# Forgetting keys, forgetting queries and memory queries by seven half-size products, zero rows in the score operands, and moved edges

## The reference, cut to what matters

```python
q_lat, c_kv, k_r, f_q, f_k, f_v, f_logit, m_q, g = jnp.split(h @ w_in, split_points, axis=-1)
...
s = jnp.einsum('bqhd,bkhd->bhqk', f_q, f_k).astype(jnp.float32) * FOX_SCALE      # forgetting branch
s = s + (jnp.swapaxes(c_q, 1, 2)[..., :, None] - jnp.swapaxes(c_k, 1, 2)[..., None, :])
...
s = jnp.einsum('bqhd,bmhd->bhqm', m_q, m_k).astype(jnp.float32) * MEM_SCALE      # memory branch
...
gates = jax.nn.sigmoid(g.astype(jnp.float32)).astype(h.dtype).reshape(b, s, N_BRANCH, D_MODEL)
...
x1 = layer_norm(ALPHA * h + mixer_out, ln1_g, ln1_b)
return layer_norm(ALPHA * x1 + moe_ffn(x1, *moe_w), ln2_g, ln2_b)
```

## Time and profile before

| what | us |
|---|---|
| median of three runs | 1115.58 |
| range of the runs | 1115.3 to 1116.18 |
| the profiled execution | 1115.3 |
| its span, first to last instruction | 1113.5 |
| PE busy in the span | 1085.7 |
| DVE busy | 494.0 |
| ACT busy | 180.4 |
| POOL busy | 87.5 |

### The profile page before, as it was taken

How to read it: one execution, slowest core, us unless ns; L and a number is a source line. 1 busy time by engine, 2 the same in 40 slices (tenths; PEclk the granted TensorE clock), 3 DMA queues, 4 the chain that set the end, 5 groups by cost and what they waited for, 6 DMA issues and landing times.

```text
span 1113.5 us, 16884 instructions
## 1 busy us (share of the span) xinstructions
PE 1085.7 (98%) x6302; PEld 655.1 (59%) x6302; DVE 494.0 (44%) x1285; ACT 180.4 (16%) x364; POOL 87.5 (8%) x103
## 2 busy tenths in 40 slices
PE   8999999999999999999999999999999999999994
PEld 4455569998777755476555545555555455555551
DVE  1130147777656333375564353343342442433435
ACT  1222124442222100010010100101101101101012
POOL 2112000000000000001034300000000000000000
PEclk9999999999999999999999999999999999999997
DMA  9632353523856578461899999999999999999971
GB/s 337 201 119 90 133 189 107 196 105 107 280 190 234 212 285 330 167 216 35 326 358 371 395 400 401 389 397 384 394 397 390 394 407 389 396 398 389 394 303 59
DMA packets 82330, 313.52 MB, mean 282 GB/s; under 512 B 13208, under 2 KB 24016, under 8 KB 56024
## 3 DMA queue, kind: packets, MB, share of 16 engines
q1 hardware_dynamic: 64864, 276.90, 63.6%
q0 software_dynamic: 7280, 16.44, 4.9%
q10 hardware_dynamic: 10128, 19.40, 4.9%
HBM read 306.24 MB, written 11.34 MB: 285 GB/s over the span
## 4 chain that ended last, share of the span: by engine, by line
PE 94%; DVE 3%; another core or an unknown queue 1%; issue 1%; ACT 0%; DMA 0%; ACTq 0%; DVEq 0%
PE ps_P L1346 20%; PE ps_V L1371 10%; PE ps_V L1360 10%; PE ps_P L1102 10%; PE ps_P L975 6%; PE ps_V L1282 6%; PE ps_S L1360 5%; PE ps_P L994 4%; PE ps_V L1291 4%; PE ps_T L1335 3%; PE ps_T L968 2%; PE ps_P L984 1%; PE ps_V L1323 1%; PE ps_P L1144 1%; PE ps_S L1353 1%
## 5 line engine op out<-in xcount | busy, mean ns | idle before, releaser
L1346 PE MATMUL ps_P<-arena,branch_out 128*64 128x256 f32 (+1 forms) x2176 | 233.6, 379 | 0.7 <-DVE branch_out L2047 0.7
L1346 PEld LDWEIGHTS ps_P<-arena,branch_out 128*64 128x64 f32 (+1 forms) x2176 | 152.0, 135 | 90.3 <-issue 19.3
L2068 DVE TENSOR_TENSOR branch_out<-branch_out,ps_P 128x256 f32<-128x256 f32 x33 | 13.9, 421 | 287.3 <-PE ps_P L1346 269.2
L1360 PE MATMUL ps_V<-weight_ring,branch_out 128*128 128x512 f32 x264 | 124.1, 592 | 0.0
L1371 PE MATMUL ps_V<-arena,branch_out 128*64 128x512 f32 (+1 forms) x544 | 120.6, 598 | 0.0
L1554 ACT ACTIVATE weight_ring<-ps_V,merge 128x512 f32<-128x512 f32 x66 | 45.3, 687 | 414.5 <-PE ps_V L1371 402.6
L2091 DVE TENSOR_TENSOR x_sb<-x_sb,ps_V 128x512 f32<-128x512 f32 x132 | 90.7, 687 | 17.4 <-PE ps_V L1360 17.2
L1371 PEld LDWEIGHTS ps_V<-arena,branch_out 128*64 128x64 f32 (+1 forms) x544 | 34.8, 135 | 77.2 <-issue 60.4
L1360 PEld LDWEIGHTS ps_V<-weight_ring,branch_out 128*128 128x128 f32 x264 | 47.9, 191 | 47.3 <-issue 47.3
L1360 PE MATMUL ps_S<-weight_ring,branch_out 128*128 128x512 f32 x132 | 67.4, 592 | 0.0
L1282 PE MATMUL ps_V<-branch_out,weight_ring 128*128 128x384 f32 x192 | 62.2, 487 | 0.5 <-DVE branch_out L1802 0.5
(11 more groups left out here) (354 smaller groups left out, 1233.4 us busy)
## 6 DMA issues: line engine op xcount, KB each, us to landing
arena<-w_e_gate SPq DMA_DIRECT2D x68, 1024.0 KB
arena<-w_e_up SPq DMA_DIRECT2D x68, 1024.0 KB
arena<-w_e_down SPq DMA_DIRECT2D x68, 1024.0 KB
weight_ring<-w_in SPq DMA_DIRECT2D x12, 1024.0 KB, 9.4
weight_ring<-w_in ACTq DMA_DIRECT2D x8, 1024.0 KB, 7.7
gates<-arena ACTq DMA_DIRECT2D x12, 384.0 KB, 3.2
arena<-fox_k_t SPq DMA_DIRECT2D x8, 512.0 KB, 3.8
arena<-cache_fox_v SPq DMA_DIRECT2D x8, 512.0 KB, 4.3
```

The lines of the kernel that those rows point to most:

```text
L1346: last = mm(bank[r:r + wide, 0:256], xgT[q][:, k, r:r + wide], w[h][:, k, :], start=(k == 0), stop=(k == KD - 1))
L1360: mm(tiles[k % 3][:, :], back[1 - q][:, (k // 2) * P:(k // 2 + 1) * P], yo[1 - q][:, (k % 2) * 512:(k % 2 + 1) * 512], start=True, stop=Tr ...
```

## The change

1. `fk`, `fq` and `mq` are computed by the same seven products as the gates: six more blocks (`HEADS_TWO`, `NH` = 6) at the front of the `W` numbering, back to back, with no attention steps between them. ACT moves each block's result to its place (`make_heads`). `fv` goes first, `fk` is feature-major at once, so `("T","fk",j)` and the DVE copies are gone; the output `fox_k` is stored feature-major from `fkA` and `fkS`, and the host turns it.
2. `inputs` runs right after the latents. The mixed inputs live in `x_sb`, so x is loaded only after the last gate product.
3. `("V","c","p")` moves from behind the `mk` transposes to between the six blocks and `qn`.
4. The rows of `krT`, `qrS`, `krTc` and of `fqA`, `fkA` that were not used are set once (zeros, and ones against zeros), and the score matmuls contract over all 128 rows. POOL does nine more clears at the start, and SP's wait `rows_set` goes from 4 to 11.
5. Half of `V out` 2 1 moves between the transposes of x1 block 0 and block 1 (`outpiece`); three eighths of `shpiece` 1 move ahead of `V rt` 1; `shact` is split in two.
6. At the end the three engines load the chunk count before their last pair, the two cases stand as `If` and `Else`, `pairs_over` is gone, the sums go in the order 0, 2, 4, 1, 3, 5 through three banks, and the first three wait for the first half of `yo` alone.

```diff
+HEADS_TWO = [(name, m) for name in ("fk", "fq", "mq") for m in range(2)]
+NH = len(HEADS_TWO)
...
-    s.append(("rms",))
-    s += [("P", "fk", j) for j in range(TT)]
+    s += [("inputs",), ("rms",)]
     s += [("P", "fv", j) for j in range(TT)]
+    s += [("weights", 0, m) for m in range(3)]
     s += [("T", "lat", j) for j in range(TT)]
-    s += [("P", "kn", 0), ("P", "kn", 1), ("P", "qr", 0), ("T", "fk", 0), ("P", "qr", 1), ("T", "fk", 1)]
-    s += [("P", "kn", 2), ("P", "kn", 3), ("T", "fk", 2), ("kcat",), ("qrope",)]
+    s += [("P", "kn", 0), ("P", "kn", 1), ("P", "qr", 0), ("P", "qr", 1), ("P", "kn", 2), ("P", "kn", 3), ("kcat",), ("qrope",)]
     s += [("P", "vm", j) for j in range(2)]
-    s += [("P", "fq", m) for m in range(4)]
+    for i in range(NH):
+        for r in range(7):
+            s.append(("W", i, r))
+            if r == 3:
+                s.append(("weights", i, 3))
+            elif r >= 4 and i + 1 < NH:
+                s.append(("weights", i + 1, r - 4))
+    s += [("V", "c", "p"), ("heads", NH - 1)]
...
-        mm(out[:, 0:keys], fqA[0:66, i, qs], fkA[0:66, i, 0:keys], start=True, stop=False)
+        mm(out[:, 0:keys], fqA[:, i, qs], fkA[:, i, 0:keys], start=True, stop=False)
...
-        mm(out[:, 0:PAST], qrS[0:RD, i, :], krTc[0:RD, :], start=False, stop=True)
+        mm(out[:, 0:PAST], qrS[:, i, :], krTc, start=False, stop=True)
...
-        last = mm(out[:, PAST:keys], qrS[0:MR, i, :], krT[0:MR, 256:T], start=False, stop=True)
+        last = mm(out[:, PAST:keys], qrS[:, i, :], krT[:, 256:T], start=False, stop=True)
...
+                if r == 0:
+                    if i == 0:
+                        pe.wait_ge(free["P"], done_at("P", "vm", 1))
...
+            def make_heads(i):
+                name, two = HEADS_TWO[i]
+                cells, ms = gate_two[i % 2], slice(2 * two, 2 * two + 2)
+                act.wait_ge(w_read, 7 * i + 7)
+                if name == "mq":
+                    last = fn(mqT[:, ms, :], cells, ACT.Copy, scale=MEM_SCALE)
+                else:
+                    heads, sample, scale = (fqA, fqS, FOX_SCALE) if name == "fq" else (fkA, fkS, 1.0)
+                    for r in range(2):
+                        fn(heads.rearrange("p (m r) c -> p m r c", r=2)[0:64, ms, r, :], cells[r * 64:(r + 1) * 64, :, 0:256], ACT.Copy, scale=scale)
+                    last = fn(sample[:, ms, :], cells[:, :, 256:T], ACT.Copy, scale=scale)
+                last.then_inc(heads_made, 1)
...
+            chunks_n = chunk_count(pe)
             step(PAIRS, 0, [(0, 32 * (PAIRS // 2 + 1)), (1, 32 * (PAIRS // 2 + 1))], quad=True)
-            with if_more(pe):
+            def last_sums(n):
+                pe.wait_ge(back_ready, n + 1)
+                pe.wait_ge(added, 6 * n + 6)
+                for m, k in enumerate(LAST_SUMS):
+                    pe.wait_ge(yo_ready, 2 * n + 1 + m // 3)
+                    if m >= 3:
+                        pe.wait_ge(last_added, m - 2)
...
+            with pe.If(chunks_n <= 4):
+                last_sums(FIXED)
+            with pe.Else():
```

More of the change, by code:

```diff
@@ L819, in _ @@
                 if n == 29:
+                    sp.wait_ge(done["W"], done_at("W", NH + TWO - 1, 6))
+                    for j in range(TT):
+                        sp.dma_start(x_sb[:, j, :], xs[j]).then_inc(x_loaded[j], 16)
                     sp.wait_ge(done["V"], done_at("V", "b", 0, 0, 0))
@@ L987, in latents @@
                             last.then_inc(done["P"], 1)
-            def feat_major(st, first, m):
-                out = bank(st)
-                for k in range(KD):
-                    if k % 4 == 0:
-                        slot = w_wait(first + k // 4)
-                    last = mm(out[:, 0:T], slot[:, k % 4, m * P:(m + 1) * P], xT[:, k, :], start=(k == 0), stop=(k == KD - 1))
-                last.then_inc(done["P"], 1)
             def scores(n):
@@ L1159, in _ @@
                         last = tr(out[0:RD, 3 * P:4 * P], kr_rot[:, j, :], P)
-                    elif key[0] == "fk":
-                        j = key[1]
-                        pe.wait_ge(free["P"], done_at("P", "fk", j))
-                        out = bank(st)
-                        for m in range(4):
-                            last = tr(out[:, m * P:(m + 1) * P], fk_tok[:, j, m * P:(m + 1) * P], P)
                     elif key[0] == "mk":
@@ L1284, in _ @@
                     elif key[0] == "out":
-                        _, j, half = key
-                        out = bank(st)
-                        for k in range(KD):
-                            pe.wait_ge(free["V"], done_at("V", "b", k // 4, 2, k % 4))
-                            if k % 4 == 0:
-                                slot = w_wait(first_of["out"] + half * 2 + k // 4)
-                            last = mm(out[:, :], yT[:, k, j * P:(j + 1) * P], slot[:, k % 4, :], start=(k == 0), stop=(k == KD - 1))
-                        last.then_inc(done["V"], 1)
+                        out_products(st, 4 if key[1:] == (TT - 1, 1) else 0, KD)
                     elif key[0] == "rt":
@@ L1566, in _ @@
                         pair(i * 2 + p + FIXED, 1 - p)
[L1567 to L1573 removed]
+                last_squares()
         @block.vector
@@ L1862, in _ @@
                 elif ring == "inputs":
[L1863 to L1865 removed]
+                    for loaded in lat_loaded:
+                        dve.wait_ge(loaded, 32)
                     x_dif, x_all, x_end, x_low = x_mix
```

272 lines of the change are left out of this document (143 added, 129 removed).

## The result

The changed kernel took 1097.21 us (median of four runs, 1096.8 to 1097.55) beside 1115.44 for the one before (four runs, 1112.93 to 1116.18); the ratio is 0.984, 95% interval 0.9823 to 0.9857. The forecast was 1097.9 with a range of 1094.5 to 1103. The profiled execution took 1096.8, its span is 1095.0 (1113.5 before): -18.5, where the steps of the prediction gave -17.65.

A forecast was written before the change was run, and what follows sets the result against it. PE was taken to bound the kernel nearly everywhere. Terms -6.4 (projections with edges), -6.3, -1.85, -3.5 and +0.4 sum to -17.65 from the profiled 1115.3 us: 1097.7, forecast 1097.9 for the runs' median, range 1094.5 to 1103.

The forecast's parts named there:

- rival E: More gain than forecast: key transposes save 1.3 us, `shd` and router waits all go, register load free; 1095.2 us, chance 0.12.
- Projections, -7.4: Key, forgetting-query and memory-query projections: 62.0 us of matmuls removed, 42 products of 1.30 us (54.6) added, without waits; -7.4 us.
- edges +1.0: Around the projections: key transposes 0, moved decay sums +0.7 at the first score, larger copies ahead of later `qn` +0.3 us.
- The +0.3 for the later `qn`: In the pattern `qn`, `mk`, `qa`: ACT's copy ahead has 512 columns instead of 384, +0.1 us three times.
- rival B: Dense projection products wait in each block for DVE or weights, 0.15 us a product, +6.3; 1104.2 us, chance 0.09.
- rival C: Projection products starve outright at 2.0 us each, making the kernel slower than before; 1127 us, chance 0.03.
- Zero rows, -6.3: First-branch scores of eight streams: full 128 rows avoid about 0.1 us on each side of every height change; 8 x -0.79.
- Rival A: Zero rows in the scores give nothing, as a switch costs on the columns' side alone; 1104.2 us, chance 0.10.
- Router, -1.85: Norm and router: second router piece 0.93 us earlier, wait at `shd` shrinks by 0.9; range -2.9 to 0.
- End, -3.5 + 0.4: Last sums start without PE's 2.09 us idle, at full clock, LN2 3.5 us earlier; PE's earlier register load costs 0.4.
- rival D: The change at the end does not pay, PE's branch stalling as long as the removed wait; 1101.4 us, chance 0.10.
- Experts, 0: Expert stage, about half the time: untouched, its loads started by PE's own progress; no change.

## Why the prediction was right, step by step

The total was 0.9 us off in the span, and the terms were right nearly one by one, with errors that cancel in part: the router gave 0.36 less, the end 0.76 more, and the first stretch 0.44 that no term had. Of rival E the free register load came true, but the key transposes saved nothing and the router less than forecast.

- **Projections, -7.4 and edges +1.0.** Measured: 62.0 removed, 54.84 added, -7.2. From the first block to the first product, keys left out, nothing changed by the chain of waits (31.27 against 51.88 - 20.60 = 31.28): the key transposes had stood where PE would have waited for ACT. The edge behind the products cost +0.77 (39.25 us from the last of them to the first score, against 38.48 without the memory queries), as much as the wait for the first score grew. The +0.3 for the later `qn` is there too (brackets of 0.26 us, and 0.11 more than before from the start of a `qa` to the next `qn`, three times), but behind the last `qa` 0.36 us went, which I had not counted. No product behind the first ever waited, so rival B and rival C are out; the added DVE work shows how far off C was. The first stretch was 0.44 shorter: 0.05 because PE's first product started at 4.24 instead of 4.29, the rest in the next few. In every profile the first four recorded instructions take about 0.75 us each and later ones of the same shape 0.36; when the faster pace sets in differs from run to run, and with it the first of the 42 products (54.42 to 55.51 in the nine profiles that share this code). What sets it off is not known, and the change need not have a part in it, since two profiles of the kernel before differ by 0.83 us there.
- **Zero rows, -6.3.** -6.24, shown alone in the old kernel. Rival A is out. My price of 0.1 us on each side of a change was right, as 0.19 a change. The 66-row products gave nothing that shows, as counted: 8 x 0.78 (1.99 - 1.31, and 0.10 at the gate product) is already the whole 6.24. The later load of x cost nothing either, since this stage, which holds the gates, takes 213.05 us with it and without.
- **Router, -1.85.** -1.49 (1.46 up to `shd` and 0.03 behind it). The step that was mis-sized is the second router piece, forecast at -0.93: it came 0.58 earlier (51.05 us behind the first output product instead of 51.63). The three shared products before it take 1.30 us, more than the wait of 0.94 that they cover, so they delay it by the difference; I had followed the transposes and not PE. The mask followed by -0.64, with a wait of 1.08 where I expected 1.3. `shd` gave -0.82 for the -0.9 expected.
- **End, -3.5 + 0.4.** -3.86, so rival D is out. PE's register load costs nothing, not 0.4. The rest is -2.16 at the first sum, where I had -2.09, and -1.70 between it and LN2, where I had about -1.4. In that second part I had reckoned with the full clock after and the low clock before, as the one profile showed; that the low clock is not always there I had not asked. So it is luck that this term came out: had the profile or the runs of before been of the other kind, it would have been 1.7 us less. On a chip where the kernel before ran at 1113.57, the changed kernel won 17.5 us instead of 18.2; whether its clock stayed up there is not known.
- **Experts, 0.** -0.08 in the first profile. This stage takes 560.7 to 561.8 us in seven profiles and 559.9 in seven others, and profiles taken together on one chip fall on the same side; the difference is a wait of up to 1.2 us in an early pair, which the rows put down to DVE. The changed kernel is found on both sides (561.09 and 559.93), but all three profiles with the projections of before are among the long ones. So it stays open whether the change makes this wait rarer; neither that nor a late arrival of weights is shown as its cause.

## What to carry to other kernels

Look at the partition heights of neighbouring float32 products: a 32-, 40- or 64-row product among full ones cost about 0.19 us for every change of class, and zero rows that bring it to 66 or more made it free. Seven half-size products back to back saved 11.6% here (54.84 us for 62.02), near the 1/8 of their columns, as long as the vector engine's fullest slot, not its mean, overran a product by no more than about half a microsecond. And cover a wait with just as much work as it is long: what stands beyond it delays the next step by the surplus, and a wait removed in a chain that another engine carries can come back as a new one, as the one before the mask did.

## What the runs showed of the hardware

- A change of row class between float32 products cost 0.19 us; 66 and 96 rows cost as 128, 64 rows among full ones as 32 or 40, and 32 beside 40 is a change too.
- The granted clock fell from 1.00 to about 0.5 behind an idle gap of 2.1 us in two of four profiles, and from the first of the last sums to LN2 it took 8.2 us instead of 6.5.
- A load of a register by PE between two dense steps or behind the last one cost no PE time; ACT's load and branch behind its last copy, and the step from there to PE, stood in the chain with 1.2 us.
- POOL took 3.92 us for an addition and 2.65 us for a product of 1024 float32 columns, with DVE passes beside both, and DVE's pass of 1.28 us beside the second took 3.05. The Trainium skill (SBUF — State Buffer, section "🔬 SBUF: two separate sides") says that a DVE operation with two inputs in SBUF and a POOL operation that reads SBUF hold a shared pair of ports in turn, and that the one that starts later is blocked for the whole instruction of the other. The trace agrees in size beside POOL's product, since the DVE pass that began 0.68 us into it ended 1.1 us behind it. It does not agree beside POOL's addition: the pass begun at 1081.98 took 1.27 us and the one begun at 1080.23, slowed to 1.82, ended 0.66 us before it (POOL's ends are rough in the profile). What decides which passes are slowed is open.
